# Softmax without scaling in the self attention: sums from the weighing, inverses by logarithm, both parts of the values from GpSimd

## The reference, cut to what matters

```
s = einsum('bqhd,bkhd->bhqk', q_i, k) * scale
s = s + c_i[..., :, None] - c_keys[:, :, None, :]      # chunked heads: s + bias
s = where(k_pos <= q_pos, s, NEG_INF)                  # chunked heads: by chunks of 64
p = jax.nn.softmax(s, axis=-1)
o = jnp.einsum('bhqk,bkhd->bqhd', p, v)
...
o_f = rms_norm(o_f.reshape(B, S, FOX_WIDTH), g_fox_out[l])
o_c = rms_norm(o_c.reshape(B, S, CHUNK_WIDTH), g_chunk_out[l])
mix = jnp.concatenate([o_f, o_c], axis=-1) @ w_out[l]
```

## Time and profile before

| what | us |
|---|---|
| median of three executions | 2093.66 |
| the three | 2092.72, 2093.66, 2097.09 |
| span of the profiled execution | 2090.6 |
| TensorE, VectorE, ScalarE, GpSimd busy in the span | 2054.0, 1120.3, 875.4, 964.1 |
| self attention, from its first score matmul to the first matmul of `mem_k` | 161.20 to 268.95 |

### The profile page before, as it was taken

One profiled execution on the slowest core, in us unless ns is written; L12 is line 12 of the kernel. 1 busy time (PEld: TensorE's weight loads), 2 busy tenths in 40 slices (PEclk: granted clock), 3 DMA queues, 4 the chain that ended last, 5 costly groups with the idle time before them and its releaser, 6 DMA issues.

```text
span 2090.6 us, 28050 instructions
## 1 busy us (share of the span) xinstructions
PE 2054.0 (98%) x9901; PEld 1688.7 (81%) x9901; DVE 1120.3 (54%) x1769; ACT 875.4 (42%) x1493; POOL 964.1 (46%) x489
## 2 busy tenths in 40 slices
PE   9999999999999999999999999999999999999997
PEld 7877787888888888787778888888777888888887
DVE  4525834335677776763385543434566635434345
ACT  5326864455222222534386322323476653232233
POOL 3437885453445545334235244444445752444443
PEclk9999999999999999999999999999999999999999
DMA  6530052214466664364323133332322031332332
GB/s 214 193 101 21 11 202 91 81 41 161 157 225 213 227 229 155 101 221 161 86 51 106 51 101 93 97 100 91 91 81 81 1 101 52 100 99 92 100 93 89
DMA packets 70325, 238.40 MB, mean 114 GB/s; under 512 B 7776, under 2 KB 11232, under 8 KB 70112
## 3 DMA queue, kind: packets, MB, share of 16 engines
q1 hardware_dynamic: 70240, 237.26, 35.4%
HBM read 231.20 MB, written 2.10 MB: 112 GB/s over the span
## 4 chain that ended last, share of the span: by engine, by line
PE 82%; DVE 6%; ACT 4%; POOL 4%; issue 3%; DMA 1%; DVEq 0%; SPq 0%; ACTq 0%; POOLq 0%
PE bank L942 25%; PE bank L944 25%; PE bank L943 25%; PE bank L1049 1%; PE bank L1176 1%; PE bank L1091 1%; POOL WL L806 1%; POOL sq L854 1%; PE bank L1064 1%; POOL t L854 1%; DVE bank L2508 1%; DVE acc L2394 1%; PE bank L1255 0%; POOL CW L879 0%; DVE x L2512 0%
## 5 line engine op out<-in xcount | busy, mean ns | idle before, releaser
L806 POOL TENSOR_TENSOR WL<-stage,WH 128x1024 fp32r<-128x1024 f32 x256 | 633.4, 2475 | 888.4 <-ACT WH L1675 883.1
L1675 ACT ACTIVATE WH<-stage 128x1024 fp32r<-128x1024 f32 x256 | 271.4, 1061 | 812.5 <-PE bank L944 799.9
L942 PE MATMUL bank<-H,WH 128*128 128x512 f32 (+1 forms) x1132 | 438.0, 387 | 2.6 <-DVE H L2418 2.1
L944 PE MATMUL bank<-H,WL 128*128 128x512 f32 (+1 forms) x1132 | 437.1, 386 | 0.0
L943 PE MATMUL bank<-H,WH 128*128 128x512 f32 (+1 forms) x1132 | 437.0, 386 | 0.0
L2757 DVE TENSOR_TENSOR Y<-bank,Y 128x512 f32<-128x512 f32 x328 | 215.6, 684 | 94.9 <-PE bank L944 94.2
L942 PE MATMUL bank<-HID,WH 128*128 128x512 f32 (+1 forms) x688 | 264.3, 384 | 0.1
L943 PE MATMUL bank<-HID,WH 128*128 128x512 f32 (+1 forms) x688 | 264.2, 384 | 0.0
L944 PE MATMUL bank<-HID,WL 128*128 128x512 f32 (+1 forms) x688 | 264.2, 384 | 0.0
L942 PEld LDWEIGHTS bank<-H,WH 128*128 128x128 f32 x1132 | 212.6, 188 | 47.9 <-issue 3.4
L944 PEld LDWEIGHTS bank<-H,WL 128*128 128x128 f32 x1132 | 212.6, 188 | 42.9
(11 more groups left out here) (468 smaller groups left out, 3612.2 us busy)
## 6 DMA issues: line engine op xcount, KB each, us to landing
stage<-panels SPq DMA_DIRECT2D x296, 512.0 KB, 3.6
ahead<-ada SPq DMA_DIRECT2D x102, 512.0 KB, 5.3
RAW<-panels SPq DMA_DIRECT2D x18, 512.0 KB, 4.0
apiece<-ada SPq DMA_DIRECT2D x10, 512.0 KB, 5.3
x<-xT SPq DMA_DIRECT2D x3, 1024.0 KB, 7.4
CS<-QKH SPq DMA_DIRECT2D x18, 128.0 KB, 2.4
outT<-x SPq DMA_DIRECT2D x16, 128.0 KB, 1.7
CS<-QKL SPq DMA_DIRECT2D x12, 128.0 KB, 2.4
```

Source lines behind the costliest of these rows:

```text
L806: pool.tensor_tensor(low_of(p, slot), stage[:, slot, :], high_of(p, slot).bitcast(F32), ALU.subtract).then_inc(s_split, 1)
L942: pe.matmul(out, wh, rh, start=start, stop=False)
L944: return pe.matmul(out, wl, rh, start=False, stop=stop)
L1675: act.activation(high_of(p, slot), stage[:, slot, :], ACT.Copy).then_inc(s_hisplit, 1)
```

## The change

The probabilities are no longer scaled. `exp` accumulates no sum, `invert` and `scale` are gone for the self attention, and `turn` waits for the exponential alone. The values are staged in a new tile VO, in which a column block of ones (64 wide) stands between the two heads' values. The stationary operand of a weighing is one head's values beside the ones, so 64 rows of the bank hold the head's result and the other 64 rows the sum of its probabilities. ScalarE takes the logarithm of those sums into the head's rows of `rstd` (`logs` for the last pair) and then, a unit later, the exponential of the negated logarithms of a pair (`inverse`). VectorE copies the head's rows to Y (`out`). Both free the bank. GpSimd multiplies Y by the inverse (`normalise`), takes over the squares (`norm_square`), and makes the high part of the values (`parts_v`) as well as the low part. VectorE's additions of squares move by a step or more, and the loads of ring panels from `mem_k` + 6 on wait for all eight `normalise`. At its start the kernel sets the ones columns (four memsets on VectorE), and the space kept for GpSimd's transfers shrinks.

```diff
+        VO = place(156, "VO", [P, 2, 2, NT, 3, CH], F32R)
...
-                return staged_v(V[:, :, u // 4 * S + u % 4 * P:u // 4 * S + u % 4 * P + P], u % 2, P)
+                src = V[:, :, u // 4 * S + u % 4 * P:u // 4 * S + u % 4 * P + P]
+                return (src.rearrange("p a (h d) -> p a h d", d=CH), VO[:, u % 2, 0, :, 0:3:2, :], VO[:, u % 2, 1, :, 0:3:2, :])
...
+        def logs_done(n):
+            return 3 * (n // 2) + n % 2 + 1
+        def inverse_done(pair):
+            return 3 * pair + 3
+        def inverse_of(pair):
+            return logs if pair == 7 else rstd
...
-            sp.wait_ge(att["self"]["out"], 16)
+            sp.wait_ge(att["self"]["normed"], 8)
...
-                    if name == "self":
-                        if s >= 12 and s % 8 == 7 and s // 8 + 1 < 8:
-                            low_v(name, s // 8 + 1)
-                        continue
...
+            def norm_square(name, m, source, width):
+                if m >= 2 or name != "mem":
+                    pool.wait_ge(s_add, first_of(ADD, name) + max(m - 1, 0))
+                pool.tensor_tensor(nsq[:, m % 2, 0:width], source, source, ALU.mult).then_inc(s_sq, 1)
+            def self_attention():
+                sm = att["self"]
+                def normalise(pair):
+                    pool.wait_ge(sm["inverted"], inverse_done(pair))
+                    pool.wait_ge(sm["out"], 2 * pair + 2)
+                    pool.tensor_tensor(Y[:, pair, :], Y[:, pair, :], inverse_of(pair)[:, :], ALU.mult).then_inc(sm["normed"], 1)
+                def head_square(name, m):
+                    pool.wait_ge(sm["normed"], m + (5 if name == "chunk" else 1))
+                    norm_square(name, m, Y[:, m + (4 if name == "chunk" else 0), :], S)
+                def parts_v(u):
+                    source, hi, _ = unit_v("self", u)
+                    if u >= 2:
+                        pool.wait_ge(sm["pv"], 8 * (u - 1))
+                    pool.tensor_copy(hi, source).then_inc(sm["v_high"], 1)
+                    low_v("self", u)
+                parts_v(0)
+                parts_v(1)
+                for s in range(64):
+                    if s >= 15 and s % 8 == 7 and s // 8 + 1 < 8:
+                        parts_v(s // 8 + 1)
+                    if s >= 16 and s % 8 == 0:
+                        normalise(s // 8 - 2)
+                    if 28 <= s < 36:
+                        if s == 28:
+                            pool.wait_ge(s_mem, 32)
+                        norm_square("mem", s - 28, memc(s - 28), MEM)
+                    if s in (36, 37, 39, 41):
+                        head_square("fox", (36, 37, 39, 41).index(s))
+                    if s in (49, 57):
+                        head_square("chunk", (s - 49) // 8)
+                for pair in (6, 7):
+                    normalise(pair)
+                    head_square("chunk", pair - 4)
...
-                    pe.wait_ge(sm["probs"], s + 1)
+                    pe.wait_ge(sm["exp" if name == "self" else "probs"], s + 1)
...
+                            pe.wait_ge(sm["inverted"], logs_done(n - 2))
...
-                    return three(O[n % 2][:, kb * P:S], VS[:, slot, 0, kb * P:(kb + 1) * P],
-                                 VS[:, slot, 1, kb * P:(kb + 1) * P], high[:, kb, kb * P:S], low[:, kb, kb * P:S],
+                    if name == "self":
+                        held = [VO[:, slot, hl, kb, n % 2:n % 2 + 2, :].rearrange("p h d -> p (h d)") for hl in range(2)]
+                    else:
+                        held = [VS[:, slot, hl, kb * P:(kb + 1) * P] for hl in range(2)]
+                    return three(O[n % 2][:, kb * P:S], held[0], held[1], high[:, kb, kb * P:S], low[:, kb, kb * P:S],
...
-                if 28 <= s < 36:
-                    if s == 28:
-                        act.wait_ge(s_mem, 32)
-                    norm_square("mem", s - 28, memc(s - 28), MEM)
-                if s in (36, 37, 39, 40):
-                    m = (36, 37, 39, 40).index(s)
-                    act.wait_ge(att["self"]["out"], 2 * m + 2)
-                    norm_square("fox", m, Y[:, m, :], S)
...
-                if s in (47, 55, 63):
-                    m = (s - 47) // 8
-                    act.wait_ge(att["self"]["out"], 2 * m + 10)
-                    norm_square("chunk", m, Y[:, 4 + m, :], S)
...
+                    if name == "self":
+                        act.activation(prob[b][:, 0:w], score_bank(name, s)[:, 0:w], ACT.Exp, bias=stat[:, b:b + 1])\
+                            .then_inc(sm["exp"], 1)
+                        return
...
-                def out(n):
+                def total_log(n):
...
-                    if name == "self":
-                        act.activation(Y[half_rows[n % 2], n // 2, :], O[n % 2][half_rows[n % 2], :], ACT.Copy)\
-                            .then_inc(sm["out"], 1)
+                    if 2 <= n < 14:
+                        act.wait_ge(sm["normed"], n // 2)
+                    act.activation(inverse_of(n // 2)[half_rows[n % 2], :], O[n % 2][half_rows[1 - n % 2], :], ACT.Ln)\
+                        .then_inc(sm["inverted"], 1)
+                def inverse(pair):
+                    act.wait_ge(sm["inverted"], logs_done(2 * pair + 1))
+                    act.activation(inverse_of(pair)[:, :], inverse_of(pair)[:, :], ACT.Exp, scale=-1.0)\
+                        .then_inc(sm["inverted"], 1)
...
-                stage_v(0)
+                if name != "self":
+                    stage_v(0)
...
-                    if s == 0:
+                    if s == 0 and name != "self":
...
+                    if name == "self" and s >= 16 and s % 8 == 0:
+                        inverse(s // 8 - 2)
...
-                            out(2 * (s // 8 - 1) + s % 2)
-                            if s % 2 and s // 8 + 1 < heads // per:
-                                stage_v(s // 8 + 1)
+                            total_log(2 * (s // 8 - 1) + s % 2)
...
-                    out(heads - 2)
-                    out(heads - 1)
+                    inverse(6)
+                    total_log(heads - 2)
+                    total_log(heads - 1)
+                    inverse(7)
...
-            act.wait_ge(att["self"]["out"], 16)
-            norm_square("chunk", 3, Y[:, 7, :], S)
...
+                    if c == 0:
+                        act.wait_ge(att["self"]["normed"], 8)
...
-                if s in (37, 39, 40):
-                    norm_add("fox", (36, 37, 39, 40).index(s), acc, S)
+                if s in (38, 40, 43):
+                    norm_add("fox", (0, 38, 40, 43).index(s), acc, S)
...
-                if s in (56, 63):
-                    norm_add("chunk", (56, 63).index(s) + 1, acc_chunk, S)
+                if s == 60:
+                    norm_add("chunk", 1, acc_chunk, S)
...
-                maximum(0)
-                maximum(1)
-                invert(0)
-                maximum(2)
-                invert(1)
-                maximum(3)
-                invert(2)
+                def out(n):
+                    rows = half_rows[n % 2]
+                    dve.wait_ge(sm["pv"], weighed(name, n, 3))
+                    dve.tensor_copy(Y[rows, n // 2, :], O[n % 2][rows, :]).then_inc(sm["out"], 1)
+                for s in range(4):
+                    maximum(s)
+                    if s and name != "self":
+                        invert(s - 1)
...
-                    if s + 3 < steps:
+                    if s + 3 < steps and name != "self":
...
+                    if name == "self" and s >= 12 and s % 8 in (6, 7):
+                        out(2 * (s // 8 - 1) + s % 2)
...
+                if name == "self":
+                    for n in range(heads_of(name) - 2, heads_of(name)):
+                        out(n)
+                    norm_add("chunk", 2, acc_chunk, S)
...
+            for slot in range(2):
+                dve.memset(VO[:, slot, 0, :, 1, :].bitcast(F32), 1.0)
+                dve.memset(VO[:, slot, 1, :, 1, :].bitcast(F32), 0.0)
...
-            dve.wait_ge(att["self"]["out"], 16)
+            dve.wait_ge(att["self"]["normed"], 8)
...
-    nc = bacc.Bacc("TRN2", target_bir_lowering=False, num_devices=1)
+    nc = bacc.Bacc("TRN2", target_bir_lowering=False, num_devices=1, dynamic_dma_scratch_size=1024)
...
```

10 lines of the change are left out of this document (3 added, 7 removed).

## The result

The changed kernel takes 2105.7 us (median of four executions, 2103.4 to 2108.3), beside 2093.4 for the kernel before on the same chip: a ratio of 1.0055, 95% interval 1.0041 to 1.0069. It is 12.3 us slower. The prediction was 2094.5, at most 2099.5, and "the same"; it was wrong.

What follows compares the result with a forecast made beforehand. TensorE was taken to bound the self attention stage, with everything behind it a chain. Loop -7.7, new wait +6.9 and clock +1.7 gave +0.9: span 2091.5, plus 3.1 to the median, 2094.5 us; range 2089.8 to 2099.5.

Steps and rivals of the forecast that it cites:

- The new wait: Before memory key panel 0: TensorE idles while the last pairs' logarithms, exponential, multiplication, square and panel low part finish; +6.9 us.
- The clock: Behind the idle gap at panel 0: granted clock falls to 0.50 for about 3.4 us, costing 1.7 us (0 to 3.4).
- The loop: Self attention loop: 10.7 us recoverable from TensorE's waits and clock, less 3.0 of waits that remain; gains 7.7 us.
- minus 3.0 remaining waits: Self attention loop: TensorE waits expected to remain after the change, five items totalling 3.0 us.
- sum of the memory squares: TensorE's sum still needs bank G[0] read by an exponential; a 0.6 us wait remains.
- steps 31 to 36: From step 31, GpSimd's values delay squares, VectorE stands, and low parts freeing transposes' banks come late; TensorE loses 1.0 us.
- steps 39 to 41: The same delay of squares behind GpSimd's values, forecast at step 39 to 40; TensorE loses 0.3 us.
- end of the loop: Transposes 62 and 63 have no scores between them, so the weighing waits for copy and low part; 0.6 us.
- small ones: Unlisted small TensorE waits remaining in the self attention loop; 0.5 us.
- Behind the stage: After self attention: everything is a chain on TensorE that shifts with the stage's end, with no further change.
- Rival B: Mid-stage VectorE becomes the bound; 7.5 us of waits remain, loop gains 3.2, kernel takes 2099 us; chance 0.25.
- GpSimd's copy: GpSimd's copy of the values (128x512) per unit, priced like the scaling of the same size at 1.58 us.

Runs made afterwards that it cites:

- the paced one: Changed kernel with panel 0 and 1 low parts ahead but after VectorE's last probabilities low part, ring panels after the loop, memory-key copy behind an earlier addition: 2096.4 us.

## Why the prediction was wrong

**The new wait (+6.9): right.** It came as one gap of 6.43 us on TensorE, released by GpSimd's low part, over the chain that the prediction listed; the square was cheaper (1.04 for 1.31), and every other link took what was forecast within 0.2 us. Ordering the low parts ahead gave back 6.0 us, of wait and clock, less the new waits it made.

**The clock (+1.7): the mechanism right, the size too small.** At panel 0, where the prediction put it, the profiles show 2.2 to 2.4 us, inside its bounds of 0 to 3.4. But filling the gap gave 5.7 us, and 4.7 on top of the later ring panels. Up to 3.5 us of the executions' time is thus tied to the idle gap and lies at no place that a profile shows. The length taken from the earlier trace rows, 3.4 us, was one case and not a constant: the run with only the smaller scratch, the kernel before in all else, has a single low stretch in the stage, of 6.8 us from 234.1 on.

**The loop (-7.7): wrong; this is the step that failed.** Of its parts, "minus 3.0 remaining waits" should have been 7.6, of which the table has 7.2 in ten waits. Against the list of the prediction, in us:

| place | forecast | measured |
|---|---|---|
| sum of the memory squares | 0.6 | 0.86 |
| steps 31 to 36 | 1.0 | 0.76 + 0.31 |
| steps 39 to 41 | 0.3 | 0.25 + 0.51 |
| end of the loop | 0.6 | 0.26 + 0.45 + 2.31 |
| small ones | 0.5 | 0.76 + 0.76 |

With 7.6 us of waits the 7.5 of before are not won back; what waits hide (by the prediction's 0.17 of each, 1.7 for these ten) stays hidden, and the low clock from 262.9 came all the same. By these terms 0.4 us are left of 10.7; the loop showed 0.8. Two things were missing. The prediction read VectorE's added load as busy time (11 us of 11.7) and not as a queue: bank O is now freed behind the low part, which is behind ScalarE's high part, which is behind a ring panel that ScalarE starts only 2.2 us earlier in the stage, where TensorE's last transposes come 3.8 earlier. With the ring panels moved the wait of 2.31 was 0.74. And it took GpSimd's and VectorE's durations from rows in which the two don't meet, though the trace of before had the addition of 2.13 us. GpSimd's low part of the values was priced as GpSimd's alone; it also costs VectorE some 1 us (1.56 for 0.50) wherever an instruction with two SBUF inputs falls upon it. With most of the values left out, two waits of 0.76 went.

**Behind the stage (nothing): wrong too.** The prediction let the stage's end carry everything behind it unchanged. TensorE waits 1.2 to 3.8 us more there in every profile with the changed code, for reasons that no run isolates. The prediction did name "a change anywhere behind the attention" as a sign of being wrong.

**Rival B** gave this mechanism (VectorE's copies, TensorE waiting for VectorE, 7.5 us of remaining waits) and 2099, with a chance of 0.25. Its waits were right; its loop gain of 3.2 was not, and the clock was too small in it as well.

**The sum**, with what was measured: +6.4 (wait) - 0.8 (loop) + 5.7 (the filled gap) = 11.3, of 12.3 us. That it comes so close is partly luck: the 5.7 is known to some 3 us, and part of it may be waits behind the stage and not clock.

**GpSimd's copy** was priced at 1.58 us by the nearest one-input row; the rows say 0.61. The prediction's estimate from the Trainium skill (GPSIMD Engine Reference, section 3.1), 0.5 to 0.8, holds it. It moved the sum by less than a microsecond.

What stays open: the profiles show 2.2 to 2.4 us of the 5.7 that the filled gap gave; where the rest lies is not shown. Nor is the cause of the added waits behind the stage, and the loop's other waits (0.25 to 0.86) were not tested one by one. And no version came below the kernel before: the paced one is 2.5 us above it (1.0012, interval from 1.0003), with waits for VectorE still in its loop, and with the copies by ScalarE it is 1.7 (1.0013).

## What to carry to other kernels

When work moves to another engine, read where the freed instruction now stands in that engine's queue and what releases the instruction ahead of it, not how busy the engine is: here TensorE waited 2.3 us for a copy of 0.68, and 1.6 of them went when the ring panels, two engines ahead, were moved. Ask of every GpSimd instruction with two SBUF inputs which of VectorE's it will lie beside. A wait of several microseconds on TensorE is priced with the clock behind it: here 2.2 us by the profile, and 4.7 to 5.7 by the times with the gap filled. And a forecast that stops at the stage's end should be checked against TensorE's idle time behind it, which here grew by up to 3.8 us.

## What the runs showed of the hardware

- VectorE's instructions with two SBUF inputs are held beside a GpSimd instruction that started first: 0.50 became 1.56 beside a low part of 1.35, and 0.69 (L2669 at 269.94) became 2.74 beside a panel's low part of 2.34. Where VectorE's started first (224.59, 0.67), GpSimd's was the longer one, 1.78 for 1.35. VectorE's that read a bank and one tile were not held (0.69 for 0.69).
- GpSimd's multiplication takes 1.29 us for 128x512 with two different tiles, 1.06 when both inputs are the same tile, and its copy 0.61.
- Around the end of a wait of 6.4 to 7.6 us TensorE's clock was at its lower level for 6.8 us (two profiles) or 10.2 (three), 1.9 to 5.4 of it in the wait, and 24 matmuls took 5.1 to 5.3 us for 2.9. Behind shorter waits in the stage it was low for nothing, 3.4 or 6.8 us. With 26 idle matmuls in the gap it stayed up.
- The same order of instructions has the low stretch at different places: the kernel before 3.4 us at 262.1, with the smaller scratch 6.8 at 234.1.
- ScalarE's logarithm and exponential follow each other with no gap (268.50 + 1.21, then 269.74).
